# A two-layer diffusion backbone on one core: shift's weights ahead of x, one sum for the squares, scale columns between block rows

## The reference

```python
m_lat = (jax.nn.silu(c) @ mod_w[layer] + mod_b[layer])[:, None, :]
m_ctx = (jax.nn.silu(c_ctx) @ mod_w[layer] + mod_b[layer])[None, None, :]
sh1, sc1, g1, sh2, sc2, g2 = jnp.split(m_lat, 6, axis=-1)
csh1, csc1, cg1, csh2, csc2, cg2 = jnp.split(m_ctx, 6, axis=-1)
u = rms_norm(h, norm_mix_w[layer]) * (1.0 + sc1) + sh1
uc = rms_norm(hc, norm_mix_w[layer]) * (1.0 + csc1) + csh1
...
z = (u @ w_in).astype(jnp.float32)
```

## Time and profile before

| what | us |
|---|---|
| median of 3 runs | 1712.6 (1711.43 to 1713.76) |
| the profiled execution, its own time | 1708.69 |
| its span, first to last instruction | 1706.9 |
| PE busy in the span | 1660.6 |

### The profile page before, as it was taken

The page is one execution under the profiler, slowest core; times in us unless marked ns, Lnnn a source line. Parts: engine busy times, 40 slices in busy tenths (PEclk is TensorE's granted clock), DMA queues, the critical chain, the costliest instruction groups (busy, mean ns, idle before and its releaser), DMA issues.

```text
span 1706.9 us, 25717 instructions
## 1 busy us (share of the span) xinstructions
PE 1660.6 (97%) x9490; PEld 1431.6 (84%) x9490; DVE 1081.3 (63%) x1699; ACT 847.6 (50%) x1410; POOL 589.4 (35%) x315
## 2 busy tenths in 40 slices
PE   7999999998999999999999999999999999999997
PEld 2777889897889999999888889986669988888876
DVE  5779976667978888888657754245774622222354
ACT  4573435776465565665334452215874433334442
POOL 0222124453244444443433432322005234444442
PEclk9999999999999999999999999999999999999998
DMA  8423223443212233333743333464224223332321
GB/s 325 144 99 114 85 100 112 133 128 136 74 63 68 87 102 88 96 102 110 286 128 122 120 114 124 142 202 145 82 76 135 74 74 99 99 98 87 99 88 60
DMA packets 71226, 197.27 MB, mean 116 GB/s; under 512 B 6322, under 2 KB 27186, under 8 KB 69826
## 3 DMA queue, kind: packets, MB, share of 16 engines
q1 hardware_dynamic: 49268, 177.29, 31.2%
q10 hardware_dynamic: 21840, 18.40, 3.6%
HBM read 187.22 MB, written 8.45 MB: 115 GB/s over the span
## 4 chain that ended last, share of the span: by engine, by line
PE 81%; DVE 12%; ACT 3%; DMA 2%; issue 1%; POOL 1%; SPq 0%; ACTq 0%; DVEq 0%; POOLq 0%
PE ps L3367 19%; PE ps L2904 18%; PE ps L3456 13%; PE ps L3012 5%; PE ps L2917 3%; PE ps L2903 3%; PE ps L3453 3%; PE ps L3317 2%; PE ps L3593 2%; PE ps L3572 2%; PE ps L3606 2%; PE ps L3018 1%; DVE raw L1787 1%; DVE left L1787 1%; DMA raw<-in_weights 1%
## 5 line engine op out<-in xcount | busy, mean ns | idle before, releaser
L819 POOL TENSOR_TENSOR wsp<-raw,wsp 128x1024 fp32r<-128x1024 f32 x141 | 358.3, 2541 | 823.0 <-ACT wsp L926 822.6
L3456 PE MATMUL ps<-hsp,wsp 128*128 128x512 f32 x984 | 276.3, 392 | 3.0 <-DVE hsp L2549 2.5
L926 ACT ACTIVATE wsp<-raw 128x1024 fp32r<-128x1024 f32 x141 | 149.6, 1061 | 245.8 <-PE ps L2904 142.4
L3456 PEld LDWEIGHTS ps<-hsp,wsp 128*128 128x128 f32 x984 | 183.5, 188 | 45.1 <-issue 4.8
L2904 PE MATMUL ps<-uf,wsp 128*128 128x512 f32 x888 | 201.4, 389 | 0.0
L2904 PEld LDWEIGHTS ps<-uf,wsp 128*128 128x128 f32 x888 | 166.7, 188 | 34.5
L3367 PE MATMUL ps<-T,wun 128*128 128x384 f32 (+1 forms) x792 | 148.5, 340 | 3.8 <-DVE ps L1943 2.5
L2904 PE MATMUL ps<-u,wsp 128*128 128x512 f32 (+1 forms) x456 | 150.8, 368 | 0.0
L3367 PEld LDWEIGHTS ps<-T,wun 128*128 128x128 f32 x792 | 141.1, 190 | 4.7 <-issue 4.1
L2917 PE MATMUL ps<-wsp,u 128*128 128x512 f32 x576 | 132.7, 391 | 3.6 <-POOL wsp L819 2.6
L2917 PEld LDWEIGHTS ps<-wsp,u 128*128 128x128 f32 x576 | 107.7, 188 | 28.3 <-POOL wsp L819 3.3
(11 more groups left out here) (366 smaller groups left out, 3221.0 us busy)
## 6 DMA issues: line engine op xcount, KB each, us to landing
raw<-in_weights SPq DMA_DIRECT2D x281, 512.0 KB, 3.6
nab<-in_nabias ACTq DMA_DIRECT2D x32, 256.0 KB, 2.8
start_w<-in_start SPq DMA_DIRECT2D x6, 1024.0 KB, 20.4
hidden_scratch<-hid0a SPq DMA_DIRECT2D x16, 384.0 KB, 4.8
hid0a<-hidden_scratch SPq DMA_DIRECT2D x5, 768.0 KB, 6.3
h<-in_x SPq DMA_DIRECT2D x4, 768.0 KB, 9.8
mD<-rows_scratch ACTq DMA_DIRECT2D x12, 256.0 KB, 4.3
mqs<-rows_scratch ACTq DMA_DIRECT2D x12, 256.0 KB, 5.3
```

The source lines that it names most:

```text
L819: pool.tensor_tensor(w[:, 1, :], raw[:, raw_index(s) % 4, :], w[:, 0, :].bitcast(F32), ALU.subtract)\
L926: act.activation(split_of(s)[:, 0, :], raw[:, raw_s % 4, :], ACT.Copy).then_inc(*own.one(hi_ready))
L3456: mm = pe.matmul(lat_of(layer, g, mm_), w, hsp[:, kk, xp, LAT], start=one, stop=last, skip_group_check=True)
```

## The change

It reorders the start and the sums in it; what is computed stays the same.

- SP's list: every shift load moves forward, the first ahead of the first x load, the last ahead of the third scale row; the fourth scale row goes behind weight block 0.
- PE sums all eight shift parts in one piece before `sums`, and the shift's transposes come before `spread`. scale_part 0 to 3 move behind block row (0,0), 4 to 7 behind (0,2), and the scale's transposes behind (0,3) and (1,0). The scale sums use PSUM bank 4, their columns bank 3.
- `sums` has one group of 12 matmuls: DVE adds all seven squares (`DIRECT` 8). It adds only square 1 before `scale_of(1)`.
- The spread of c makes the context half first, and each half signals its own end, so DVE's first multiply waits for one half only.
- DVE makes raw rows 0, 1 and 2 before it takes the shift columns; then come low row 0, scale_of(3), low row 1, raw row 3, low rows 2 and 3.

```diff
-        DIRECT = (KT - 1, KT - 1, KT - 1, KT - 1, 5)
+        DIRECT = (KT, KT - 1, KT - 1, KT - 1, 5)
...
-            return (0, 1, 2, 6)[n], n // 2, slice(512 * (n % 2), 512 * (n % 2) + 512)
+            return (0, 1, 2, 6)[n], 1 - n // 2, slice(512 * (n % 2), 512 * (n % 2) + 512)
...
             load_scale(0)
+            load_shift(0)
             load_x(0)
+            load_shift(1)
             load_x(1)
             load_scale(1)
-            load_shift(0)
+            load_shift(2)
             load_x(2)
             load_x(3)
+            load_shift(3)
             load_scale(2)
-            load_shift(1)
+            load(raw_index(0))
             load_scale(3)
-            load_shift(2)
-            load_shift(3)
-            load(raw_index(0))
...
-            sp.wait_ge(c_ready.sem, 1)
+            sp.wait_ge(c_ready.sem, 2)
...
-                   .then_inc(*own.one(c_ready if n == C_SPREAD - 1 else act_own))
+                   .then_inc(*own.one(c_ready if n % 2 else act_own))
...
                 for col in (1, 0):
+                    dve.wait_ge(c_ready.sem, 2 - col)
...
                 raw_row(0)
                 raw_row(1)
+                raw_row(2)
                 dve.wait_ge(start_columns.sem, SH_TURNED)
...
-                raw_row(2)
+                low_row(0)
+                scale_of(3)
+                low_row(1)
                 raw_row(3)
-                for k in range(SC_ROWS):
-                    low_row(k)
+                low_row(2)
+                low_row(3)
...
-            dve.wait_ge(c_ready.sem, 1)
             scale_of(0)
-            for k in (1, 2, 3):
-                add_squares(norm[0], k, slice(0, N_TOK))
+            add_squares(norm[0], 1, slice(0, N_TOK))
             scale_of(1)
-            for k in (4, 5, 6):
+            for k in range(2, KT):
                 add_squares(norm[0], k, slice(0, N_TOK))
             scale_of(2)
-            scale_of(3)
...
-            for k in range(4):
+            for k in range(KT):
                 shift_part(k)
             sums(norm[0], slice(0, N_TOK))
-            shift_part(4)
-            shift_part(5)
             pe.wait_ge(ident_loaded.sem, 16)
-            spread(norm[0], slice(0, N_TOK))
-            shift_part(6)
-            shift_part(7)
             pe.wait_ge(start_rows.sem, SHROW_READY)
             for k in range(KT):
                 mm = pe.transpose(ps[:, 3, 2 * k:2 * k + 2], shrow[0:2, tile(k)], ident[0:2, 0:2])
             mm.then_inc(*own.one(start_columns))
-            for k in range(4):
-                scale_part(k)
+            spread(norm[0], slice(0, N_TOK))
...
             first_row(0, 0)
-            for k in range(4, KT):
+            for k in range(4):
                 scale_part(k)
             first_row(0, 1)
             first_row(0, 2)
+            for k in range(4, KT):
+                scale_part(k)
+            first_row(0, 3)
+            first_row(1, 0)
             pe.wait_ge(start_rows.sem, SCROW_READY)
...
-            first_row(0, 3)
-            for k in range(4):
+            for k in range(1, 4):
                 first_row(1, k)
```

More of the change, by code:

```diff
@@ L417, in build @@
         row_ready = sem("row_ready")
-        DIRECT = (KT - 1, KT - 1, KT - 1, KT - 1, 5)
-        N_ADDED = (KT - 2, KT - 2, 3 + 2 * 3, 3 + 2 * 3, 4)
+        DIRECT = (KT, KT - 1, KT - 1, KT - 1, 5)
+        N_ADDED = (KT - 1, KT - 2, 3 + 2 * 3, 3 + 2 * 3, 4)
         N_SQUARED = (KT, KT, 4 + 2 * 4, 4 + 2 * 4, KT)
-        N_SUMMED = (2, 2, 2 * 2, 2 * 2, 4)
+        N_SUMMED = (1, 2, 2 * 2, 2 * 2, 4)
         TURN = (1, 2, 3, 5, 7)
@@ L1121, in _ @@
             act.wait_ge(start_columns.sem, SC_DONE)
-            act.activation(shrow[0:2, 0:512], ps[0:2, 7, :], ACT.Copy).then_inc(*own.one(start_rows))
+            act.activation(shrow[0:2, 0:512], ps[0:2, 4, :], ACT.Copy).then_inc(*own.one(start_rows))
             high_parts(norm[0], shift(0, 0), all_tokens, range(SC_ROWS, KT))
@@ L2062, in first_operand @@
                    .then_inc(*own.one(sh_ready))
-                raw_row(2)
+                low_row(0)
+                scale_of(3)
+                low_row(1)
                 raw_row(3)
-                for k in range(SC_ROWS):
-                    low_row(k)
+                low_row(2)
+                low_row(3)
                 n = KT - SC_ROWS
                 dve.wait_ge(start_columns.sem, SC_TURNED)
-                dve.tensor_tensor(modm[:, KT + SC_ROWS:2 * KT, :], ps[:, 4, 0:2 * n].rearrange("p (k r) -> p k r", r=2),
+                dve.tensor_tensor(modm[:, KT + SC_ROWS:2 * KT, :], ps[:, 3, 0:2 * n].rearrange("p (k r) -> p k r", r=2),
                                   sc_one[:, SC_ROWS:KT].unsqueeze(2).to_broadcast([P, n, 2]), ALU.add)\
@@ L2942, in scale_part @@
                     pe.wait_ge(sc_loaded[4 + k // 4].sem, 16)
-                mm = pe.matmul(ps[0:2, 7, :], vec[:, V_CCOL + 2 * k:V_CCOL + 2 * k + 2],
+                mm = pe.matmul(ps[0:2, 4, :], vec[:, V_CCOL + 2 * k:V_CCOL + 2 * k + 2],
                                start_w[:, 0, SC_ROWS + k // 2, 512 * (k % 2):512 * (k % 2) + 512],
@@ L2988, in _ @@
             first_row(0, 2)
+            for k in range(4, KT):
+                scale_part(k)
+            first_row(0, 3)
+            first_row(1, 0)
             pe.wait_ge(start_rows.sem, SCROW_READY)
             for k in range(KT - SC_ROWS):
-                mm = pe.transpose(ps[:, 4, 2 * k:2 * k + 2], shrow[0:2, tile(k)], ident[0:2, 0:2])
+                mm = pe.transpose(ps[:, 3, 2 * k:2 * k + 2], shrow[0:2, tile(k)], ident[0:2, 0:2])
             mm.then_inc(*own.one(start_columns))
-            first_row(0, 3)
-            for k in range(4):
+            for k in range(1, 4):
                 first_row(1, k)
```

## The result

The changed kernel takes 1719.81 us (median of 7 runs, 1717.62 to 1723.1) against 1712.86 us (7 runs, 1711.43 to 1716.51) of the kernel before on the same chip: +6.95 us, a ratio of 1.004 with a 95% interval of 1.003 to 1.005: 0.4% slower, clear of the noise. The forecast was 1720.5, the range 1715.0 to 1724.0.

A forecast was written before the change was run, and what follows sets the result against it. The prediction took PE, busy 97% of the span, to bound the kernel, so start delays carry to the end. 4.0 at full clock + 1.7 + 2.15 of clock = 7.85 us on 1712.6 gives 1720.5, range 1715.0 to 1724.0.

The forecast's parts named there:

- Loads and shift in one piece: Start of PE: last shift load lands at 25.9, PE waits 2.7 us, parts 6 and 7 run 26.0 to 29.5.
- First pause: PE's 2.7 us wait before shift's last load: half clock for 3.4 us of work afterwards, 1.7 us lost.
- second rival: Clock falls behind neither PE pause: 4.0 us later, 1716.6; chance 0.10.
- first rival: PE's wait before shift's last load costs no clock: 6.15 us later, 1718.7; chance 0.22.
- Row (0,0): First block row on PE: starts at 41.1 against 42.94 at full clock, 1.8 us earlier.
- Second pause: PE's 6.4 us idling between spread and (0,0): 2.5 us of clock lost in (0,0) and scale parts, 2.15 net.
- Scale parts behind (0,0): Four parts cost PE 3.5 us; scale's transposes come at 54.4, 4.4 us later; sum at full clock 4.0 us later.
- Block 0: Yardstick, the moment ACT takes the first finished block: 63.17 before, forecast near 71, 7.85 us later.
- collisions go: After 103 us, four DVE instructions held up by POOL, 8.4 us in all, run free: 1712.1, no change; chance 0.10.
- faster: Kernel gains by something unseen; row (0,0) would have to start at 37.1; chance 0.06.
- the clock stays up in both: Neither PE pause, before shift's last load or before (0,0), costs clock: 4.0 us later, 1716.6; chance 0.10.
- First pause harmless: PE's wait before shift's last load leaves the clock alone: 7.85 - 1.7 = 6.15 us later, 1718.7; chance 0.22.

The follow-up runs named there:

- run 4: Changed kernel with 3 extra matmuls after shift part 5 and 4 after spread, results unread, to fill PE's pauses: 1719.88 us against 1712.74 for the kernel before.
- run 11: Changed kernel with 3 extra matmuls after shift part 5 and 6 after spread, results unread: 1718.50 us against 1712.65 for the kernel before.
- run 3: Changed kernel with scale parts 0 to 3 back ahead of (0,0) and scale_of(3) moved to DVE's wait for spread: 1718.03 us against 1712.74 before.
- run 6: Changed kernel with raw row 2 put back behind the shift columns: 1721.72 us against 1713.11 for the kernel before.
- run 1: Changed kernel with scale parts 0 to 3 put back ahead of block row (0,0): 1719.91 us against 1712.74 for the kernel before.
- run 2: Changed kernel with scale_of(3) moved from between the low rows to DVE's wait for spread: 1721.49 us against 1712.74 for the kernel before.
- run 5: Kernel before with only scale parts 0 to 3 moved behind block row (0,0): 1716.49 us against 1713.11 unedited.
- run 7: Kernel before, unchanged, profiled a second time: 1712.79 us against 1713.11, block 0 taken at 64.92.
- run 8: Changed kernel, PE and DVE lists reordered: sums ahead of shift parts 6 and 7, all scale parts ahead of (0,0): 1709.51 us against 1713.11 before.
- run 9: The kernel of run 8 with four extra matmuls filling PE's wait before sums: 1706.75 us against 1712.73 for the kernel before.
- run 10: The kernel of run 8 with the loads in the old order and sums behind shift part 3: 1709.76 us against 1712.73 for the kernel before.

## Why the prediction was right

- **Loads and shift in one piece.** Forecast: last load at 25.9, a wait of 2.7, parts 6 and 7 from 26.0. Measured: 25.52, 2.68, 25.53. The addition of the seventh square was hidden as said.
- **First pause, 1.7 us of clock.** Measured 1.43 (5.02 less 3.59). Runs 4 and 11, where the pause was filled and the parts took 3.60, fit it as the cause. But the loss isn't certain: with the same pause left in (2.66 to 2.68), the parts took 5.02, 4.96 and 5.29 in the changed kernel and runs 3 and 6, and 3.59 in runs 1 and 2. That the forecast had it in this profile is in part luck. The Trainium skill ("TensorE: Matmul & The Clock Gate", section "Why this matters for your kernels") would allow a pause of this length between bursts; that holds in runs 1 and 2 and fails in the changed kernel and in runs 3 and 6. The prediction names the second rival's sum for this; with only the first pause free it is the first rival's, 1718.7.
- **Row (0,0).** Forecast 41.1 at full clock, 42.8 with the first loss. Measured 42.27: 0.4 of the difference is the earlier landing, 0.3 the smaller loss; spread's 0.39 at the lower clock works against them.
- **Second pause, 2.5 us of clock.** The mis-sized term, and the step that failed. (0,0) lost 1.0 (2.19 to the parts against 1.22) and the first scale parts 0.5 (4.09 against 3.59): 1.5. The clock had fallen at 35.5 and not after the pause, and so was up again at 45.7, before the parts were through. Place right, size wrong, and the cause too, as far as one profile tells: the low level began before this pause. In runs 4 and 11, where the pause was cut to 2.56 us or filled, the clock was still lost, at other places.
- **Scale parts behind (0,0), transposes 4.4 us later at full clock.** Measured 6.6 with the clock's 1.43 + 0.39 + 1.5 in it, which leaves 3.3; the landing 0.4 earlier and the 0.35 us wait for low row 2, which the slow parts covered, close most of the gap. Run 5 shows the mechanism by itself.
- **Block 0.** Forecast 7.85 later, 71.0; measured 6.2 later, 69.36. Of the 1.65 between them, 0.55 are the start and 1.0 the second pause's clock. The 6.2 consist of these, to 0.2 us: 3.5 of scale parts behind (0,0), 1.5 of clock there, 1.7 of waits for row 4 and those behind it (forecast 1.1 + 0.3 + 0.35), less the 0.7 by which (0,0) came earlier.
- **The end.** Forecast +7.85 on the median; measured +6.95, within 1 us. Nothing up to 150 us gave the loss back: the four long DVE instructions behind the earlier trace rows are all still held up by POOL (2.78, 3.42, 3.85 and 3.19 us, from 109.75 to 136.5), and the next one is 6.4 us later than before (144.55 against 138.18). The 0.2 us that the prediction adds where POOL's split meets DVE's last modulation product came as 0.4: the split at 71.56 took 2.72, against 2.34 before. Of the rivals, "collisions go", "faster" and "the clock stays up in both" fell. "First pause harmless", forecast at 1718.7, happens in some executions, as runs 1 and 2 show, and lies as near to the measured median as the forecast does. How often each happens can't be told from one profile a kernel.
- **What stays open.** The two profiled executions differ by 10.6 us and the medians by 6.95. Run 7's profile is 6.0 us longer than that of the same kernel shown before, 1.75 of it at block 0 and the rest in later stretches. So a difference that arises behind block 0 between two single profiles can't be put down to the change, and I didn't trace it further. At block 0 too, the change reads +6.2 against one profile of before and +4.4 against the other. The kernel before loses clock in its start in some executions, which the prediction put at nothing when it added 7.85 to a median. That the end came out within 1 us of the forecast, nearer than block 0 did, is in part luck.

## What to carry to other kernels

Work that stands in an engine's wait is free only there. PE sets the time here, so four scale parts cost their whole 3.5 us, and clock beside it, once they stood behind the wait (run 5). Before moving such work, ask also what hangs on its result: the scale's transposes feed DVE's whole second half, and 6.6 us late they added some 1.7 us of waits. Two moves can each be cover for the other, so undo them together and not only one by one. And before cutting a piece out, look which pauses it leaves on TensorE: the three starts that beat the kernel before (runs 8, 9 and 10) have all eight scale parts in what was PE's wait and no pause from `spread` to (0,0). The one with the lowest median has four useless matmuls in its last pause.

## What the runs showed of the hardware

- A fall of the clock came behind a pause of only 1.65 us (spread 2.93 in place of 1.60, in runs 1, 2, 6 and 11), and the same pause in run 4 was followed by none there (1.60). The length of a pause doesn't decide alone: behind 2.66 to 2.68 us the same eight records took 4.96 to 5.29 in three executions and 3.59 in two.
- Where matmuls filled one pause, the fall came at another (runs 4 and 11). Where no other long one was left (run 9), the clock stayed up, for 1.75 us at block 0 in one profile each.
- DVE instructions with two inputs in SBUF that began while POOL was splitting a block took about 2 us more, wherever they were put. The raw rows, whose second input lies in PSUM, didn't: in the changed kernel three of them took 3.49 from 36.21 on, 1.16 each as before, though POOL was splitting until 37.07, and in run 9 two took 2.31 beside a whole split (44.65 to 46.96, POOL 44.69 to 47.08). The timeline of DVE in run 9 shows the first multiply of scale_of(3), which takes 1.23 elsewhere, and that of POOL the split beside it:

```profile
30.01 3.03 DVE L2024 SCALAR_TENSOR_TENSOR left<-start_w,c_both 128x1024 f32<-128x1024 f32 x1
```

```profile
29.62 2.35 POOL L819 TENSOR_TENSOR wsp<-raw,wsp 128x1024 fp32r<-128x1024 f32 x1 [28.76 <-ACT wsp L926]
```

The multiply ends at 33.04, 1.07 us after POOL's end at 31.97, which is about its own length: it did its work only when POOL was through. The Trainium skill ("SBUF — State Buffer", section "Who interferes with whom") says that the two share a port that one holds alone; the rows agree. A piece "hidden" in DVE's wait pays this price when POOL splits a block at the same time: scale_of(3) held the first raw row back to 34.57, while spread had ended at 33.09.
